# Cross-attention by split products in a two-layer SSD / sliding-window encoder: fp32 scores and values replaced by three fp32r products each, a residual load and two gate products moved

## The reference

```
def memory_cross_attention(q_flat, mem_kv):
    q  = q_flat.reshape(b, s, MEM_HEADS, MEM_HEAD_DIM)            # 512 tokens, 4 heads of 128
    mk = mem_kv[..., :MEM_WIDTH].reshape(b, -1, MEM_HEADS, MEM_HEAD_DIM)   # 256 memory tokens
    mv = mem_kv[..., MEM_WIDTH:].reshape(b, -1, MEM_HEADS, MEM_HEAD_DIM)
    sc = einsum("bshd,bmhd->bhsm", q, mk) * MEM_HEAD_DIM ** -0.5
    p  = softmax(sc, axis=-1)
    return einsum("bhsm,bmhd->bshd", p, mv).reshape(b, s, MEM_WIDTH)
...
for i in range(DEPTH):
    mem_kv = rmsnorm(mem, mem_norm[i]) @ w_mem_kv[i]
    proj   = rmsnorm(h, norm_mix_pre[i]) @ w_in[i]
    y      = concat([mixer(proj[..., :n]), memory_cross_attention(proj[..., n:], mem_kv)])
    h      = h + rmsnorm(y @ w_out[i], norm_mix_post[i])
    h      = h + rmsnorm(mlp(rmsnorm(h, norm_mlp_pre[i])), norm_mlp_post[i])
```

## Time and profile before

| | |
|---|---|
| three timed executions | 1273.62, 1275.49, 1275.60 us, median 1275.49 |
| profiled execution | 1274.03 us, its span 1272.3 us |
| TensorE's granted clock, mean | 0.998 |
| busy PE / DVE / ACT / POOL | 1262.5 / 908.7 / 737.4 / 161.9 us |

### The profile page before, as it was taken

The page is one execution under the profiler, slowest core; times in us unless marked ns, Lnnn a source line. Parts: engine busy times, 40 slices in busy tenths (PEclk is TensorE's granted clock), DMA queues, the critical chain, the costliest instruction groups (busy, mean ns, idle before and its releaser), DMA issues.

```text
span 1272.3 us, 19420 instructions
## 1 busy us (share of the span) xinstructions
PE 1262.5 (99%) x7607; PEld 1083.4 (85%) x7607; DVE 908.7 (71%) x1236; ACT 737.4 (58%) x1249; POOL 161.9 (13%) x195
## 2 busy tenths in 40 slices
PE   9999999999999999999999999999999999999998
PEld 7787878888778989999888898777789999988886
DVE  5676775988633786777787974776467776868987
ACT  6645355677542655567565753775464566665663
POOL 0046354363000000000000000000000000000000
PEclk9999999999999999999999999999999999999999
DMA  8488776352765357949976527656227378579854
GB/s 276 148 271 268 242 170 170 109 170 85 208 149 140 106 225 208 230 143 221 259 248 195 185 81 168 129 117 150 82 68 234 133 181 232 193 218 250 251 179 151
DMA packets 110386, 230.29 MB, mean 181 GB/s; under 512 B 8134, under 2 KB 18646, under 8 KB 110038
## 3 DMA queue, kind: packets, MB, share of 16 engines
q1 hardware_dynamic: 84240, 159.93, 38.3%
q0 software_dynamic: 21760, 67.11, 24.2%
q10 hardware_dynamic: 4294, 2.00, 0.8%
HBM read 225.69 MB, written 70.04 MB: 232 GB/s over the span
## 4 chain that ended last, share of the span: by engine, by line
PE 98%; DVE 1%; DMA 0%; issue 0%; ACT 0%; SPq 0%; DVEq 0%; ACTq 0%
PE G L2291 34%; PE G L2779 5%; PE G L2781 5%; PE G L2783 5%; PE X L2742 4%; PE X L2740 4%; PE X L2738 4%; PE X L2314 3%; PE X L2779 3%; PE X L2783 3%; PE X L2781 3%; PE X L2376 3%; PE G L2376 3%; PE G L2740 3%; PE G L2738 3%; PE G L2742 3%
## 5 line engine op out<-in xcount | busy, mean ns | idle before, releaser
L1326 ACT ACTIVATE whi<-raw 128x1024 fp32r<-128x1024 f32 x112 | 118.2, 1058 | 107.5 <-PE G L2783 41.3
L2050 DVE TENSOR_TENSOR wlo<-raw,whi 128x1024 fp32r<-128x1024 f32 x112 | 135.3, 1221 | 48.8 <-ACT whi L1326 48.6
L1522 DVE TENSOR_TENSOR wlo<-raw,whi 128x1024 fp32r<-128x1024 f32 x77 | 94.7, 1230 | 91.2 <-ACT whi L828 91.1
L1244 ACT ACTIVATE whi<-raw 128x1024 fp32r<-128x1024 f32 x84 | 88.9, 1061 | 103.3 <-PE X L2742 52.0
L2291 PE MATMUL G<-uhi,whi 128*128 128x512 f32 x352 | 144.9, 412 | 0.3 <-DVE ulo L1539 0.2
L1983 DVE TENSOR_TENSOR wlo<-raw,whi 128x1024 fp32r<-128x1024 f32 x84 | 102.7, 1223 | 58.0 <-ACT whi L1244 57.5
L2291 PE MATMUL G<-uhi,wlo 128*128 128x512 f32 x352 | 137.7, 391 | 0.0
L2291 PE MATMUL G<-ulo,whi 128*128 128x512 f32 x352 | 137.3, 390 | 0.0
L828 ACT ACTIVATE whi<-raw 128x1024 fp32r<-128x1024 f32 x77 | 81.5, 1058 | 81.8 <-PE G L2291 33.4
L730 POOL DMA_DIRECT2D tsum<-in_w_down x32 | 32.9, 1038 | 624.3 <-PE G L2291 328.8
L2779 PE MATMUL G<-whi,left_hi 128*128 128x512 f32 x224 | 87.3, 390 | 0.0
(11 more groups left out here) (421 smaller groups left out, 3629.1 us busy)
## 6 DMA issues: line engine op xcount, KB each, us to landing
tsum<-in_w_down POOLq DMA_DIRECT2D x48, 1024.0 KB, 10.2
raw<-in_w_up SPq DMA_DIRECT2D x64, 512.0 KB, 6.1
raw<-tsum SPq DMA_DIRECT2D x64, 512.0 KB, 4.4
raw<-in_w_down SPq DMA_DIRECT2D x48, 512.0 KB, 4.9
raw<-in_ssd_w_out SPq DMA_DIRECT2D x16, 512.0 KB, 4.4
raw<-in_swa_w_in SPq DMA_DIRECT2D x16, 512.0 KB, 4.5
csrow<-cs_rows SPq DMA_DIRECT2D x16, 384.0 KB, 4.6
raw<-in_swa_w_out SPq DMA_DIRECT2D x12, 512.0 KB, 3.9
```

Of the source, the lines that this page charges most:

```text
L1244: act.activation(whi[n % 4][:, :, :], up_right(g, r, q), ACT.Copy).then_inc(hi_done, up_fill(g, k))
L1326: act.activation(whi[n % 4][:, :, :], down_raw[n % 4][:, :, :], ACT.Copy).then_inc(hi_done, 1)
L1522: dve.tensor_tensor(wlo[q][:, :, :], src[:, :, :], whi[q][:, :, :].bitcast(F32), ALU.subtract).then_inc(lo_done, 1)
L2050: dve.tensor_tensor(wlo[n % 4][:, :, :], down_raw[n % 4][:, :, :], whi[n % 4][:, :, :].bitcast(F32), ALU.subtract).then_inc(lo_done, 1)
```

## The change

The scores and the values of both layers become three fp32r products of split operands, accumulated in one bank. What this needs:
- K, V and the query heads are split (`part_hi` on ScalarE, `part_lo` on VectorE). In layer 0 K and the first two heads just ahead of the stage, V in step 0, heads 2 and 3 in steps 1 and 2; in layer 1 K and V ahead of the query projection, heads 0 and 1 at slots 33 to 37, heads 2 and 3 in steps 1 and 2.
- The transposed probabilities too: ScalarE's copy now writes the high part, and `turned_lo` on VectorE subtracts it from B[2]. TensorE waits for this one (`ma_pT_lo`) before it transposes into B[2] again, and before it uses the values.
- The new tiles take the place of h's first half until the stage of layer 0 is over, so the residual's load moves behind the last value product (`ma_o`), ahead of the load of panel 64.
- `z_out` of the first gate block's banks 0 and 1 stands ahead of the scan's `unit_within` in VectorE's queue, behind it before.
- Some semaphores are merged; their waits stay the same. Some tiles move within SBUF.

```diff
+PARTS = (("K", 0, 1, "V", 2, 3), ("K", "V", 0, 1, 2, 3))
+Q_PARTS = (33, 35)
...
@@ sync: load of W_out of layer 0
                     if (j, q) == (0, 7):
-                        sp.wait_ge(s_cb, UNITS)
-                        sp.wait_ge(panel_done, 4 * B_W0)
+                        sp.wait_ge(y_tr, 12)
+                        gains("norm_mix_post", "norm_mlp_pre", 0, 0)
+                    elif (j, q) == (1, 3):
+                        sp.wait_ge(ma_o, MH)
                         for t in range(NT):
                             sp.dma_start(h[:, t, :], x_rows[t]).then_inc(h_in, 16)
-                        sp.wait_ge(y_tr, 12)
-                        gains("norm_mix_post", "norm_mlp_pre", 0, 0)
...
@@ scalar
+            def part_hi(i, what):
+                whole, hi_part, _ = part_of(i, what)
+                act.activation(hi_part, whole, ACT.Copy).then_inc(ma_part_hi, 1)
...
                 act.wait_ge(ma_tr, 8 * i + n + 1)
-                act.activation(mpT[h % 2][:, :, 256 * tp:256 * tp + 256],
+                act.activation(mpT[0][h % 2][:, :, 256 * tp:256 * tp + 256],
                                B[2][:, :].rearrange("p (m n) -> p m n", m=MT), ACT.Copy).then_inc(ma_pT, 1)
+                if n == 0 and i == 0:
+                    part_hi(i, "V")
+                elif n in (1, 2):
+                    part_hi(i, n + 1)
...
@@ vector
+            def part_lo(i, what):
+                whole, hi_part, lo_part = part_of(i, what)
+                dve.wait_ge(ma_part_hi, part_count(i, what))
+                dve.tensor_tensor(lo_part, whole, hi_part.bitcast(F32), ALU.subtract).then_inc(ma_part_lo, 1)
+
+            def turned_lo(i, mpT, B, n):
+                h, tp = divmod(n, 2)
+                cols = slice(256 * tp, 256 * tp + 256)
+                dve.wait_ge(ma_pT, 8 * i + n + 1)
+                dve.tensor_tensor(mpT[1][h % 2][:, :, cols], B[2][:, :].rearrange("p (m n) -> p m n", m=MT),
+                                  mpT[0][h % 2][:, :, cols].bitcast(F32), ALU.subtract).then_inc(ma_pT_lo, 1)
...
-            def memory_step(i, mp, yh, yl, B, n, next_panel):
+            def memory_step(i, mp, mpT, yh, yl, B, n, next_panel):
                 h, tp = divmod(n, 2)
                 j = 2 * n
+                if n > 0:
+                    turned_lo(i, mpT, B, n - 1)
                 if n + 1 < 2 * MH:
                     maxima(i, B, n + 1)
...
+                if n == 0 and i == 0:
+                    part_lo(i, "V")
+                elif n in (1, 2):
+                    part_lo(i, n + 1)
...
@@ vector, panel(p)
+                if p == 4 * B_Z[0] + 3:
+                    z_out(0, (0, 1))
                 if v is not None:
                     unit_within(v)
...
@@ tensor, memory_scores
-                    mm = pe.matmul(B[tp][:, M * t:M * t + M], q[:, h, rows], memKT[i][:, h, :],
-                                   start=True, stop=True)
+                    o = B[tp][:, M * t:M * t + M]
+                    pe.matmul(o, q[0][:, h, rows], k_hi, start=True, stop=False)
+                    pe.matmul(o, q[1][:, h, rows], k_hi, start=False, stop=False)
+                    mm = pe.matmul(o, q[0][:, h, rows], k_lo, start=False, stop=True)
...
@@ tensor, memory_values
-                pe.wait_ge(ma_pT, 8 * i + 2 * h + 2)
+                pe.wait_ge(ma_part_lo, part_count(i, "V"))
+                pe.wait_ge(ma_pT_lo, 8 * i + 2 * h + 2)
...
+                    pe.matmul(B[3][:, :], v_hi, p_hi, start=(mt == 0), stop=False)
+                    pe.matmul(B[3][:, :], v_hi, p_lo, start=False, stop=False)
+                    mm = pe.matmul(B[3][:, :], v_lo, p_hi, start=False, stop=(mt == MT - 1))
...
@@ tensor, memory_step
-                    pe.wait_ge(ma_pT, 8 * i + n)
+                    pe.wait_ge(ma_pT_lo, 8 * i + n)
```

More of the change, by code:

```diff
@@ L92, with part_count @@
 GATE_AT = {36: 0, 39: 1, 43: 2}
+PE_REL, PE_DT, PE_DT_TURNED, PE_CS, PE_CS_TURNED = 1, 2, 3, 6, 7
+PARTS = (("K", 0, 1, "V", 2, 3), ("K", "V", 0, 1, 2, 3))
+def part_count(i, what):
+    return 6 * i + PARTS[i].index(what) + 1
 def conv_of(g):
@@ L305, in build @@
         state = put("state", [P, SR, HD], F32, 90)
-        mp0 = [put(f"mp0{i}", [P, 2, M], F32, U_AT + 24 + 2 * i) for i in range(2)]
-        mpT0 = [put(f"mpT0{i}", [P, MT, T], F32, U_AT + 4 * i) for i in range(2)]
+        mp0 = [nc.alloc_sbuf_tensor_at(f"mp0{i}", [P, 2, M], F32, offset=ht_at + 8192 + 2048 * i)
+               for i in range(2)]
+        mpT0 = [[put(f"mpT0hi{i}", [P, MT, T], F32R, 40 + 4 * i) for i in range(2)],
+                [nc.alloc_sbuf_tensor_at(f"mpT0lo{i}", [P, MT, T], F32R, offset=ht_at + 4096 * i)
+                 for i in range(2)]]
+        qm0 = (put("qm0hi", [P, MH, T], F32R, U_AT), put("qm0lo", [P, MH, T], F32R, U_AT + 16))
+        mem_hi0 = put("mK0hi", [P, MH, M], F32R, U_AT + 28), put("mV0hi", [P, MT, MH * P], F32R, U_AT + 24)
         ymhi0 = put("ymhi0", [P, MH, T], F32R, 72)
@@ L353, in build @@
               for i in range(2)]
-        mpT1 = [put(f"mpT1{i}", [P, MT, T], F32, 116 + 4 * i) for i in range(2)]
+        mpT1 = [[put(f"mpT1hi{i}", [P, MT, T], F32R, 116 + 4 * i) for i in range(2)],
+                [put(f"mpT1lo{i}", [P, MT, T], F32R, U_AT + 4 * i) for i in range(2)]]
+        qm1 = (put("qm1hi", [P, MH, T], F32R, 80), put("qm1lo", [P, MH, T], F32R, 16))
+        mem_hi1 = put("mK1hi", [P, MH, M], F32R, 72), put("mV1hi", [P, MT, MH * P], F32R, 76)
+        memK = [(mem_hi[0], nc.alloc_sbuf_tensor_at(f"mK{i}lo", [P, MH, M], F32R, offset=kv_at + 4096 * i))
+                for i, mem_hi in enumerate((mem_hi0, mem_hi1))]
+        memVs = [(mem_hi[1], nc.alloc_sbuf_tensor_at(f"mV{i}lo", [P, MT, MH * P], F32R, offset=kv_at + 8192 + 4096 * i))
+                 for i, mem_hi in enumerate((mem_hi0, mem_hi1))]
         bias = nc.alloc_sbuf_tensor_at("bias", [P, 8, P], F32, offset=kv_at)
@@ L362, in build, with part_of @@
         mem_raw = raw + [put(f"mem_raw{x}", [P, 2, 512], F32, U_AT + 4 * x) for x in range(2)]
+        def part_of(i, what):
+            if what == "K":
+                return [memKT[i][:, :, :]] + [x[:, :, :] for x in memK[i]]
+            if what == "V":
+                return [memV[i][:, :, :]] + [x[:, :, :] for x in memVs[i]]
+            return [x[:, what, :] for x in ((qmT0,) + qm0, (qmT1,) + qm1)[i]]
         def raw_of(blk, q):
@@ L1089, in mixer_out_panel @@
                 if q == 0:
+                    for what in ("K", 0, 1):
+                        part_hi(0, what)
                     ahead(*todo)
@@ L1484, in attention_panel @@
                     ahead(*todo)
+            for what in ("K", "V"):
+                part_hi(1, what)
             ahead(B_QA)
@@ L1764, in panel @@
                     silu_pair(*silu)
[L1765 removed]
+                if p % 4 == 3 and p // 4 in B_Z[1:]:
                     z_out(B_Z.index(p // 4), (0, 1))
@@ L1802, in mixer_out_panel @@
                 if q == 0:
+                    for what in ("K", 0, 1):
+                        part_lo(0, what)
                     ahead(*todo)
@@ L2171, in _ @@
             link(dve.tensor_scalar(sinkb[:, 1, :], sinkb[:, 0, :], -1.0, None, ALU.mult))
+            for what in ("K", "V"):
+                part_lo(1, what)
             dve.wait_ge(bias_in, 32)
```

69 lines of the change are left out of this document (39 added, 30 removed).

## The result

The changed kernel takes 1280.37 us (median of 6 runs, 1279.77 to 1283.93), the one before 1275.28 (6 runs); the ratio on record is 1.0053, 95% interval 1.0042 to 1.0064. The two medians are 5.1 us apart, a quotient of 1.0040; the record doesn't say how its ratio weighs the executions, so the slowdown is 5 to 7 us, where 7.6 were predicted. The profiled execution took 1280.39 us, its span is 1278.6: 6.3 more than before's. What follows explains these 6.3 us, one execution of each kernel.

What follows compares the result with a forecast made beforehand. TensorE's work plus its waits was taken to bound the kernel: 1274.0 - 5.2 + 7.4 + 4.6 - 0.2 + 1.0 = 1281.6 us, put at 1282 for the timed runs; 8 in 10 range 1276 to 1287.

Steps and rivals of the forecast that it cites:

- The products' saving: Scores and values in both layers' cross-attention: 16 x 0.15 + 8 x 0.35 = 5.2 us saved; ends 4.5 and 6.9.
- The chain of 3.61 us: Cross-attention: copy, subtraction, maxima and normalising product in series take 3.61 us from one step's transposes to the next's.
- Layer 1's waits: Layer 1's cross-attention: added TensorE waits of 1.08, 2.16, 0.79, 1.6 and 1.80, sum 7.4 us, bounds 6.5 and 8.
- Layer 0, 4.6 us: Layer 0's cross-attention: late y tiles 10 and 11, steps 1, 2 and 5 to 6 add 4.6 us; bounds 2.5 and 6.
- The gate banks: First gate banks, ahead of panel 12's first matmul: a TensorE wait of 0.2 us goes; between -0.4 and 0.
- The residual: Residual's four 512 KB loads, moved ahead of panel 64's load, delay the last panels: +1.0 us, bounds 0 and 4.
- The step from 1281.6 to 1282: Whole kernel: sum raised to 1282 because executions of the kernel before lie around 1274.8, its profiled one at 1274.0.
- the likeliest case: Whole kernel: all chains as worked out, 68%; own range 1277.5 to 1287 us.
- Faster: Rival, cross-attention: the subtraction never delays the normalisation, chain under about 2.5 us; 1269.4 us, 11%.
- No change: Rival, both attentions: waits half of those forecast (6 us of 12) and the residual costs nothing; 1275 us, 12%.
- Much slower: Rival, last four panels: the residual's transfers starve them, one load late, +5 beyond forecast; 1287 us or more, 7%.
- The clock falls: Rival, layer 1's attention, 870 to 908: pauses drop TensorE's clock to 1.2 GHz, another 38 us; about 1320, 2%.

Runs made afterwards that it cites:

- e9_early: e2_splits with VectorE's order product of n, maxima of n+1, subtraction of n-1; two layer-0 subtractions behind y tiles, layer-1 panel work moved: 1273.26 us.
- e10_early_plain: e9_early with one plain fp32 product of the high parts in place of each three fp32r products: 1276.49 us, ratio 1.0016.
- e1_order: Changed kernel with VectorE's subtraction for step n-1 moved behind the maxima of n+1 and the normalising product of n: 1278.39 us, ratio 1.0030.
- e3_both: Changed kernel with both the subtraction moved behind maxima and product and the splits moved out of the steps: 1272.06 us, ratio 0.9983.
- e7_twice: Changed kernel with VectorE reading bank X2 once more (0.69 us) ahead of each subtraction: 1287.10 us, ratio 1.0105.
- e2_splits: Changed kernel, same subtraction order, with the splits of V and query heads 2 and 3 moved away from the copies: 1277.52 us, ratio 1.0020.
- e12_joined: Layer 1 as in e9_early; layer 0 with maxima first, except products of steps 1 and 2, and later splits of heads 2 and 3: 1270.72 us, ratio 0.9966.
- e4_moves: Kernel before with only the gate products moved forward and the residual's loads moved behind the last value group: 1273.31 us, ratio 0.9992.
- e6_plain: e3_both with VectorE's normalising product one step earlier and one plain fp32 product of high parts for each three: 1276.57 us, ratio 1.0014.

## Why the prediction was right, point by point

- **The products' saving, 5.2 us: right.** e9_early against e10_early_plain gives 0.13 to 0.16 for a score group and 0.35 for a value group, that is 16 x 0.145 + 8 x 0.35 = 5.1. By the rule of four passes for plain fp32 (the Trainium skill, FP8 and Floating Point Precision, TensorE Precision Notes) the prediction's estimate was 6.9; the pair disagrees with it, in the same way as the starts of the earlier trace rows did.
- **The chain of 3.61 us: right, to the last link.** Steps 0 to 1 and 5 to 6 take 3.61 in the trace. Layer 1's waits by starts, with the predicted values behind them: 1.08 (1.08), 2.25 (2.16), 0.88 (0.79), 1.49 (1.6), 1.80 (1.80); sum 7.5 (7.4). e1_order, e3_both and e7_twice show the cause from both sides: take the subtraction out of the maxima's way and the waits go, lengthen it and they grow by 3.3.
- **Layer 0, 4.6 us: right in sum.** +1.88 net is 4.5 of waits less 2.6 of products. By starts tile 11 is 1.88 late (1.8), tile 10 0.77 (0.9), step 5 to 6 0.40 (0.4). e2_splits shows that the splits inside the stage make 2.7 of the 4.5; of the rest e12_joined takes another 1.1 off the stage by the order of the queue.
- **The gate banks, -0.2: right, a little small.** The first matmul of panel 12 starts 0.23 behind the one ahead of it, as the next pair shows, 0.44 in the earlier trace rows; a microsecond later another 0.09 is gone, so -0.30, in each of the kernels with this edit.

```profile
86.27 0.40 PE L2372 MATMUL G<-wlo,uhi 128*128 128x512 f32 x1
86.50 0.39 PE L2372 MATMUL G<-uhi,whi 128*128 128x512 f32 x1
```

- **The residual, +1.0: mis-sized, it is 0.** The last conversion of the stretch and the square behind it, which answer to the earlier trace rows, and the stretch's totals, which answer to the earlier trace rows:

```profile
398.82 1.06 ACT L863 ACTIVATE whi<-raw 128x1024 fp32r<-128x1024 f32 x1 [5.17 <-DMA raw<-in_ssd_w_out]
403.40 0.60 ACT L1184 ACTIVATE junk<-X 128x512 f32<-128x512 f32 x1 [3.52 <-PE X L2395]
```

```profile
372.00:400.00 28.00, 28.00 (x125) 23.20 (x124) 8.88 (x11) 9.43 (x15) 2.03 (x2) 1.00 1.02 279
```

The load is 1.41 us later where TensorE is 1.05 later, so 0.4 of the 1.1 us of slack is used and nothing more. The step that failed is "at the stretch's own rate ... 230 at full": the queues moved 279 GB/s once there was more to move. I had seen that the rate was pulled down by the sums, and still took a quarter of the bound. e4_moves shows no change of offset there either.
- **What the sum did not have: +0.78, -0.55 and -0.30.** In the changed kernel a weight load of layer 0's down projection comes late, 220 us behind the attention:

```profile
624.27 1.06 ACT L1372 ACTIVATE whi<-raw 128x1024 fp32r<-128x1024 f32 x1 [0.59 <-DMA raw<-tsum]
...
627.45 0.50 PE L2868 MATMUL G<-whi,left_hi 128*128 128x512 f32 x1 [0.39 <-DVE wlo L2125]
```

ScalarE's conversion waits for the load, and VectorE's `wlo` stands behind two operations of its own. By the offsets such loads cost 0.6 to 2.8 us in 8 of the 14 profiled executions of this study, at about 612 to 630 or at 1174 to 1197, none in the others. They come with offsets at 600 us of -2.7, -1.1 and +1.1, and are absent at -1.7, -0.9, +1.1 (e6_plain) and +3.1, so it isn't a matter of phase alone. What makes them late was not settled. The -0.55 arises in the first 12 us, where every profiled execution here differs from before's by 0.1 to 0.6; the -0.30 at 1168 is a short wait that before's had and most others hadn't. None of these is in the prediction's sum. It came out 1.3 us too high: 1.0 is the residual, 0.2 the attentions and the gate, and the three terms that it lacks happen to cancel; that is luck. The step from 1281.6 to 1282 took it that the timed executions lie above the profiled one, as they did before; the changed kernel's median is its profiled execution's 1280.4. The bounds of the likeliest case don't follow closely from its terms either: these give about 1277 and 1288, and 1277.5 and 1287 were taken.
- **The rivals.** "Faster" named its point: the chain under about 2.5 us. e9_early reaches it in layer 1 and e12_joined is faster, by 4.5 of the 5.4 us of that rival; the changed kernel's queue isn't so ordered. "No change" needed half of the waits; the trace has all of them, 7.5 and 4.5 us. "Much slower" needed a late load in the last four panels; none is late there. "The clock falls" did not happen in the changed kernel and did, for 3.4 us, in e7_twice.

## What to carry to other kernels

When a step gets a new operation, write down the engine's queue between two turns of the bottleneck engine and sum from one turn to the next; an engine that is busy half of the time can still set the pace, and its place in the queue decides more than its length (the same operations gave 28.0 and 20.8 us for one stage). Put what waits longest last, never let a queue stop for a result that it needs only in the next turn, and move work without a deadline out of the steps. Measure what an operation costs on TensorE only where TensorE doesn't wait.

## What the runs showed of the hardware that I had not expected

- TensorE's clock fell for a few microseconds in the midst of the kernel: granted 0.55 and 0.60 on average from 909 to 911 and 911 to 913 us in e7_twice, and 1.00 again at 913; it cost 1.6 us. Ahead of it TensorE had paused by the brackets for 1.51, 1.80, 1.28, 1.87, 0.16 and 2.22 us within 24 us. Pauses up to 1.61 us, five in the same stretch of the changed kernel, left it at 1.00, and no other of the 14 profiled executions has such a fall. The Trainium skill (TensorE: Matmul & The Clock Gate, A second HAM failure mode) tells of short idle gaps between groups of matmuls that make the clock go back and forth; the trace of e7_twice agrees as far as one fall and return go, that of the changed kernel doesn't.
- The DMA queues moved 279 GB/s, at 1.02 busy, in a stretch that had shown 189 GB/s at 0.82; the share of busy time did not tell what room was left.
- The waits view's sums come short: 6.7 + 2.2 us for transposes and tiles, where starts give 7.5 + 4.5 for the two stages.
